# A fifth buffer for split expert weights, with the hand-overs of ScalarE and VectorE one unit on

## The reference

```
logits = h @ w_router;  top_v, top_i = top_k(logits, 2);  gates = softmax(top_v) at top_i
for e in range(8):
    y = y + gates[:, e] * ((silu(h @ w_gate[e]) * (h @ w_up[e])) @ w_down[e])     # 1024 x 3584 each
x = x + y;  return rmsnorm(x, final_norm)
```

## Time and profile before

| | us |
|---|---|
| median of 3 runs | 1400.06 (1399.85 to 1401.4) |
| the profiled execution | 1399.72 |
| its span | 1397.99 |
| TensorE busy in the span | 1367.6 (98%) |
| TensorE's granted clock | 0.998 |

### The profile page before, as it was taken

The page is one execution under the profiler, slowest core; times in us unless marked ns, Lnnn a source line. Parts: engine busy times, 40 slices in busy tenths (PEclk is TensorE's granted clock), DMA queues, the critical chain, the costliest instruction groups (busy, mean ns, idle before and its releaser), DMA issues.

```text
span 1398.0 us, 16748 instructions
## 1 busy us (share of the span) xinstructions
PE 1367.6 (98%) x6662; PEld 1058.6 (76%) x6662; DVE 1103.1 (79%) x858; ACT 925.5 (66%) x723; POOL 51.2 (4%) x51
## 2 busy tenths in 40 slices
PE   9999999999999999999999999999999999999997
PEld 7886788887988888756788866678876668886654
DVE  4786644456455998898998888998888999988898
ACT  3566543344454777777877777787777787777775
POOL 1000000000010000000000000000000000002000
PEclk9999999999999999999999999999999999999999
DMA  9744465555642899999999999999999999999994
GB/s 312 221 157 148 162 210 180 181 180 166 211 149 79 324 361 400 367 376 405 380 406 394 371 390 373 411 383 415 383 358 395 386 399 398 396 381 376 413 403 161
DMA packets 136643, 439.14 MB, mean 314 GB/s; under 512 B 11520, under 2 KB 28912, under 8 KB 120816
## 3 DMA queue, kind: packets, MB, share of 16 engines
q1 hardware_dynamic: 130688, 424.24, 81.1%
q0 software_dynamic: 3392, 12.07, 2.5%
q10 hardware_dynamic: 2480, 1.69, 0.4%
HBM read 432.20 MB, written 5.78 MB: 313 GB/s over the span
## 4 chain that ended last, share of the span: by engine, by line
PE 80%; DVE 15%; ACT 2%; issue 2%; DMA 1%; ACTq 0%; DVEq 0%
PE ps L1879 25%; PE ps L1881 24%; PE ps L1880 24%; DVE lo L1203 9%; PE ps L2427 2%; DVE work L1668 1%; DMA work<-bias_by_distance 1%; PE ps L1939 1%; PE ps L2364 1%; PE ps L2365 1%; DVE work L1229 0%; ACT hi L782 0%; DMA bias_by_distance<-diag_sb 0%; PE ps L2175 0%; DVE x L1657 0%
## 5 line engine op out<-in xcount | busy, mean ns | idle before, releaser
L1203 DVE TENSOR_TENSOR lo<-raw,hi 128x2048 fp32r<-128x2048 f32 (+1 forms) x403 | 903.8, 2282 | 99.9 <-ACT hi L782 98.4
L782 ACT ACTIVATE hi<-raw 128x2048 fp32r<-128x2048 f32 (+1 forms) x403 | 769.1, 1915 | 242.1 <-PE ps L1881 208.2
L1879 PE MATMUL ps<-hi,xT_hi 128*128 128x512 f32 (+2 forms) x1200 | 470.8, 392 | 5.0 <-DVE lo L1203 3.6
L1881 PE MATMUL ps<-hi,xT_lo 128*128 128x512 f32 (+2 forms) x1200 | 465.6, 388 | 0.0
L1880 PE MATMUL ps<-lo,xT_hi 128*128 128x512 f32 (+2 forms) x1200 | 465.4, 388 | 0.0
L1879 PEld LDWEIGHTS ps<-hi,xT_hi 128*128 128x128 f32 (+1 forms) x1200 | 201.7, 168 | 80.7 <-issue 6.9
L1881 PEld LDWEIGHTS ps<-hi,xT_lo 128*128 128x128 f32 (+1 forms) x1200 | 201.4, 168 | 71.4
L1880 PEld LDWEIGHTS ps<-lo,xT_hi 128*128 128x128 f32 (+1 forms) x1200 | 201.6, 168 | 66.7
L1879 PE MATMUL ps<-hi,hT_hi 128*128 128x512 f32 x296 | 116.1, 392 | 0.0
L1881 PE MATMUL ps<-hi,hT_lo 128*128 128x512 f32 x296 | 115.3, 390 | 0.0
L1880 PE MATMUL ps<-lo,hT_hi 128*128 128x512 f32 x296 | 115.2, 389 | 0.0
(11 more groups left out here) (312 smaller groups left out, 942.9 us busy)
## 6 DMA issues: line engine op xcount, KB each, us to landing
raw<-in_od_w_gate_dram SPq DMA_DIRECT2D x112, 1024.0 KB, 8.2
raw<-in_od_w_up_dram SPq DMA_DIRECT2D x112, 1024.0 KB, 8.8
raw<-in_od_w_down_dram SPq DMA_DIRECT2D x112, 1024.0 KB, 8.2
raw<-in_od_w_qkv_dram SPq DMA_DIRECT2D x12, 1024.0 KB, 5.3
raw<-in_ev_w_gate_dram SPq DMA_DIRECT2D x11, 1024.0 KB, 5.3
raw<-in_ev_w_up_dram SPq DMA_DIRECT2D x11, 1024.0 KB, 5.1
raw<-in_ev_w_down_dram SPq DMA_DIRECT2D x11, 1024.0 KB, 5.2
raw<-in_ev_w_in_dram SPq DMA_DIRECT2D x4, 1024.0 KB, 11.0
```

Of the source, the lines that this page charges most:

```text
L782: act.activation(unit(hi, n), unit(raw, n), ACT.Copy).then_inc(hi_ready, 1)
L1203: dve.tensor_tensor(unit(lo, n), unit(raw, n), unit(hi, n).bitcast(F32), ALU.subtract)\
L1879: pe.matmul(out, s_hi, m_hi, start=start, stop=False, skip_group_check=True)
L1881: return pe.matmul(out, s_lo, m_hi, start=False, stop=stop, skip_group_check=True)
```

## The change

The fifth slot (`hi4`, `lo4`) fills the arena. It is used in the branch with gathered tokens; `moe_slots[0]` is set back to 4 while the code of the dense branch is written out. Every `used(k)` of that branch now issues the splits one unit further, on ScalarE and on VectorE, so that each hand-over stands one split later in their orders. The four fetched results go to other rows: the free half of `gain`, `probT`, and two parts of `work`, which held the gathered rows and the stored result. GpSimd waits for one count more (`gathered`, 16) before it fetches. In the dense branch `hd` moves to the first two of these rows.

```diff
@@ constants @@
 HM = 4
+SM = 5
@@ build @@
+    moe_slots = [SM]
+
     def slot_of(n):
-        return n % H if n < U_MOE else (n - U_MOE) % HM
+        return n % H if n < U_MOE else (n - U_MOE) % moe_slots[0]
 
     def frees_slot(n):
         if n < U_MOE:
             return n - H + 1
-        if n >= U_MOE + HM:
-            return n - HM + 1
+        if n >= U_MOE + moe_slots[0]:
+            return n - moe_slots[0] + 1
+        if slot_of(n) == H + 1:
+            return U_MOE
         if slot_of(n) == H:
             return U_WO[1] + 1
...
+        hi4 = nc.alloc_sbuf_tensor_at("hi4", [P, UNIT], F32R, offset=arena_at)
+        lo4 = nc.alloc_sbuf_tensor_at("lo4", [P, UNIT], F32R, offset=arena_at + 4 * UNIT)
...
-        hd = nc.alloc_sbuf_tensor_at("hd", [P, T, D], F32, offset=arena_at)
...
-        results = nc.alloc_sbuf_tensor_at("results", [P, 2 * T, D], F32, offset=arena_at)
+        probT_row = probT[:].rearrange("p t h q -> p (t h q)")
...
-            if slot_of(n) == H:
-                return (hi3 if ring is hi else lo3)[:, 0:a * b]
+            if slot_of(n) >= H:
+                return ((hi3, hi4) if ring is hi else (lo3, lo4))[slot_of(n) - H][:, 0:a * b]
...
         def result_row(i):
-            return results[:, i, :]
+            return (gain[:, 1, :], probT_row, work[:, 2, :], work[:, 3, :])[i]
@@ gpsimd @@
                 pool.wait_ge(slots_ready, 1)
+                pool.wait_ge(gathered, 2 * NE)
                 pool.wait_ge(y_stored, stores_before(NE - 1))
@@ scalar, gathered branch @@
                     def used(k):
-                        splits_to(min(first_of(e) + k + 3, U_END))
+                        splits_to(min(first_of(e) + k + 4, U_END))
@@ vector, gathered branch @@
                     def used(k):
-                        splits_to(min(first_of(e) + k + 2, U_END))
+                        splits_to(min(first_of(e) + k + 3, U_END))
@@ scalar, vector, tensor @@
+            moe_slots[0] = HM
             with act.Else():
...
+            moe_slots[0] = SM
```

More of the change, by code:

```diff
@@ L601, in scatter_bank, with dense_h @@
             return 2 + i if e == NE - 1 else 6
-        def dense_h(c):
-            return hd if c % 2 else work[:, 2:4, :]
+        def dense_h(c, t):
+            return (gain[:, 1, :], probT_row)[t] if c % 2 else work[:, 2 + t, :]
         VARS = [1, 4, 6, 8, 10]
@@ L1839, in dense_pair @@
                             for t in range(T):
-                                dve.tensor_tensor(dense_h(c)[:, t, 0:w], work[:, t, 0:w],
+                                dve.tensor_tensor(dense_h(c, t)[:, 0:w], work[:, t, 0:w],
                                                   ps[:, 4 + 2 * t:4 + 2 * t + w // W, :].rearrange("p a n -> p (a n)"),
@@ L2519, in dense_down @@
                                         ins = pe.transpose(ps[:, 4 + t, P * j:P * j + P],
-                                                           dense_h(c)[:, t, W * b + j:W * b + W:4], ident[:])
+                                                           dense_h(c, t)[:, W * b + j:W * b + W:4], ident[:])
                                 ins.then_inc(hT_done, 1)
```

## The result

| | before | after |
|---|---|---|
| median of each | 1400.73 us (1399.85 to 1403.35, 4 runs) | 1390.05 us (1389.86 to 1391.95, 4 runs) |
| ratio, with its 95% interval | | 0.992 [0.9908, 0.9932] |
| profiled execution, its span | 1399.72, 1397.99 | 1391.95, 1390.1 |
| expert stage in it (end of the last unit before it to the last down matmul) | 445.56 to 1386.44: 940.88 | 449.65 to 1378.59: 928.94 |

The four executions of before are the three known ahead of the prediction and one more, of 1403.35 us. 12.0 was predicted.

A forecast was written before the change was run, and what follows sets the result against it. TensorE, busy 98% of the span, was taken as the bound, losing time to VectorE's late low parts. Gains of 8.9, 2.3 and 0.8 us made 12.0, so 1400.06 became 1388.0 us, range 1385.5 to 1397.

The forecast's parts named there:

- What can be won: Expert stage, 459 to 1386 us: TensorE's lost time sums to 11.8 us, at most 13.3 with uncounted hand-overs.
- The size: Experts 1, 3, 5 and three starts win 8.9 us, expert 7 2.3, small hand-overs 0.8: 12.0.
- Neither works alone: Expert stage: neither the fifth buffer with old orders nor the new orders with four buffers works.
- The head start comes from each split being one unit ahead: Expert stage, buffer and orders together: each split comes one unit ahead, 2.72 to 2.76 us, or 1.81 after a down.
- Part 2, the product behind one more subtraction: VectorE's last product in half-tile experts, behind one more subtraction, stays free: 0, bounds 0 to 2.2 us each.
- Part 3, the results' rows and GpSimd's wait: Results in other rows and one more GpSimd wait before the fetches: cost 0, with 50 us of room.
- The loads have room: Expert stage: weight loads keep up at 414 GB/s, with 10 us to spare per pair of experts.
- The first rival: Expert stage: loads become the bound in part and halve the stage's gain, 1391 to 1397 us; chance 0.17.
- the second, that nothing moves: Queue engines are full, so earlier issue only lengthens the queue: 1399 to 1401 us; chance 0.08.
- The slower rival: Moved hand-overs block ScalarE and VectorE, some 3.6 us per half-tile expert: 1402 to 1412 us; chance 0.08.

The follow-up runs named there:

- Experiment 3: Kernel after with four buffers instead of five, both ScalarE's and VectorE's orders one unit on: 1394.66 us, ratio 0.9948.
- experiment 5: Kernel after with four buffers and ScalarE's hand-overs as before, only VectorE's order one unit on: 1395.1 us, ratio 0.9958.
- 2: buffer: Kernel after with both engines' hand-overs put back, so five buffers and the results' new rows alone: 1401.23 us, ratio 0.9995.
- experiment 6: Kernel after with VectorE's hand-overs put back, so five buffers and ScalarE's order alone one unit on: 1408.52 us, ratio 1.0056.
- 4: VectorE, five: Kernel after with ScalarE's hand-overs put back, so five buffers and VectorE's order alone one unit on: 1391.0 us, ratio 0.9926.
- experiment 8: Kernel before with VectorE subtracting only half of each expert-stage unit from the fifth on, all orders kept: 1387.85 us, ratio 0.9905.
- 9: Kernel after with each expert-stage load bringing only the first half of its unit: 1389.56 us, ratio 0.9916.
- 7: Five buffers, ScalarE's order alone one unit on, each expert-stage load bringing only half its unit: 1401.08 us, ratio 0.9998 to before.
- experiment 1: Kernel after run again unchanged, on two chips: 1389.83 us, ratio 0.9913, and 1389.59 us, ratio 0.9918.
- the fill: Kernel after with extra TensorE matmuls at two waits in layer 0, six near 34 us and two at 134 us: 1388.58 us, ratio 0.9916.

## Why the prediction was right, and where its reasons were not

How far ahead of TensorE the parts of a unit are, in expert 3, shows which engine mattered. Each number is the end of the last matmul of the unit before, less the end of the subtraction (low) or split (high) of this unit, from the timelines; a low part at or below 0 means that TensorE waits or comes without a margin. Experiment 3 has the numbers of 5 to within 0.02.

| | before | 2: buffer | 6: ScalarE | 5: VectorE, four | 4: VectorE, five | after |
|---|---|---|---|---|---|---|
| low, first gate unit of chunk 3 | -0.01 | -0.03 | -0.04 | 0.16 | 1.62 | 1.62 |
| low, third down unit of chunk 3 | -0.63 | -0.62 | -0.63 | 1.65 | 2.47 | 3.10 |
| low, first unit of expert 4 | -0.03 | -0.03 | -0.03 | -0.03 | 0.17 | 0.80 |
| high, third down unit of chunk 3 | 5.16 | 5.19 | 7.00 | 5.16 | 5.20 | 7.00 |
| time, us | 1400.7 to 1401.8 | 1401.23 | 1408.52 | 1395.1 | 1391.0 | 1389.6 to 1390.05 |

- *What can be won: right.* 11.8 and at most 13.3 were counted from the starts of matmuls; the floor that experiment 8 shows lies 13.38 below before. The difference to 11.8 is mostly expert 7: it had 112.36 - 108.51 = 3.85 to lose, where the prediction found 2.9. The rest is about 0.1 in each of the other half-tile experts and in expert 0, and 0.18 at the starts.
- *The size: right.* Predicted 8.9 and 2.3 and 0.8, together 12.0; measured in the stage 11.94. Expert 1 won 3.21 (3.1), 3 and 5 won 2.41 each (2.3), 7 won 2.40 (2.3 of its 2.9), the starts 0.46 each (0.4). What the stage gave beyond 11.2 is 0.74, for which 0.8 had been taken from between 0 and 1.5: that it came so close is luck, and so in part are the 2.3 of expert 7, taken from between 0 and 2.9. The time itself came 2.05 us above 1388.0. The stage accounts for 0.06 of that: the rest is the clock in layer 0 (up to 3.6 us between executions), and the 1400.06 that I set out from was the low end of what before does (1400.73, 1401.83, 1401.52 and 1401.02 as medians of later sets).
- *"Neither works alone": wrong.* This is the step that failed. The buffer alone does nothing, as said. But the orders alone give 6.8 us of the stage, and VectorE's alone gives the same (3, 5). I had costed the new orders by ScalarE, by the ring and by the silu behind it, and had not asked what VectorE's own order does. The rows were there: in the earlier trace rows VectorE idles 1.21 us before the product at 904.51. The next high part was ready before that: ScalarE was last in front of this unit at 901.81 for 1.92 us, so from 903.73 on.

```profile
901.81 1.92 ACT L782 ACTIVATE hi<-raw 128x2048 fp32r<-128x2048 f32 x1 [0.84 <-PE ps L1881]
```

  (ScalarE's timeline in the kernel before.) VectorE began that unit at 905.64. The head start of low parts was limited by VectorE's order and not by the buffers alone; with five buffers it was the order entirely (2).
- *The head start comes from each split being one unit ahead: wrong in its cause.* The table shows that ScalarE's high parts one unit ahead (5.16 to 7.00) give the low parts nothing by themselves (6), and with VectorE's shift only the last 0.63 (4 against after). Added in this sequence, VectorE's order gives 6.75 of the stage's 11.94 us (940.88 to 934.13), the fifth buffer under it 4.28 (to 929.85), and ScalarE's order 0.91 (to 928.94); in another sequence the shares differ, since the buffer first gives 0.25. The right size came from the right sum of waits, and from the right bound (one unit more covers a lack of 1.8), with the wrong engine named. That the total did not need the right engine is luck too: both parts were changed together.
- *Part 2, the product behind one more subtraction: right.* The product starts with the same 1.21 us of idle time before it, so the extra subtraction was done earlier, as said.
- *Part 3, the results' rows and GpSimd's wait: right.* The first fetch is still released by a store, after 7.91 us of waiting (7.60 in the earlier trace rows), so the added wait had long been met:

```profile
1278.48 1.31 POOL L773 DMA_INDIRECT gain<-expert_results,rslot_id  x1 [7.91 <-DMA expert_results<-work]
```

- *The loads have room: right.* They moved at 391 and 397 GB/s in experts 2 and 3, which is 394 over the pair, where 394 had been worked out as needed, ScalarE's waits for them grew as foretold, and halving them changed nothing (9). The first rival is out, and with 10.7 to 12.0 us won so is the second, that nothing moves. The Trainium skill (DMA: Bandwidth & Descriptors, Where 436 GB/s comes from) says that some 358 GB/s per core bind for loads from HBM. The 397 over 109.6 us speak against that for this kernel, which runs on one core. The Trainium skill (HBM Reference, Specifications (TRN2)) says that a core that streams alone measures well above this share. The trace agrees with that, by the same 397.
- *The slower rival: a real mechanism, with the wrong trigger.* I put it where VectorE's product meets one more subtraction and gave it 3.6 us per half-tile expert. It happened where ScalarE stands before a load with a copy of h behind it, in full-tile experts above all, and only if VectorE is not shifted too (6, 7). In the kernel after ScalarE has such waits as well, up to 2.2 us in the execution shown and 2.9 in another, and they cost nothing: they add up to less than half of those in experiment 6, and wherever outside expert 7 one exceeds 0.3 us, the low part of that unit is still done 1.8 us or more before TensorE is through with the unit before. In expert 7 halved loads changed nothing (9). So ScalarE's shift needs VectorE's, and not the other way round (4).

## What to carry to other kernels

Where one engine feeds another through a ring, three numbers bound the head start: the buffers, and the place in the order of each engine that works ahead; count all three, and look for idle time that an engine spends in front of an in-order step while its next independent piece is ready. Here a buffer without the order behind it gave nothing (2), and moving the first engine of the chain alone cost 5.6 us of the stage (6): it wanted its input earlier, and that input's buffer is only freed by the second one. And a program that leaves half of one engine's work out, with every order kept, gives the floor in one run; it is better evidence for the cause than a sum of small waits.

## What was not expected of the hardware

TensorE's granted clock fell to 0.50 in layer 0 in nine of the fourteen profiled executions, and not in others of the same kernel on the same data. At the first place, before the matmuls with `flip` at 35 us, TensorE had waited 1.94 and 1.76 us in the kernel after, 1.80 in experiment 5 and 2.43 in experiment 6 where it fell. It stayed at 1.00 after 1.63 us in the kernel after, but also after 2.01 us in experiment 8, whose layer 0 has the same instructions. So the length of the wait alone doesn't decide it. At the second place, from 133.6 us on, it fell in six executions. In the twelve without the fill a wait of 0.55 us after the matmuls of L2083 stands there, in five with the fall and in seven without; the sixth fall came with the fill. In eight of the nine executions a stretch lasted 3.4 us, in experiment 3 one of 6.8. By the starts in the table of experiment 1 one of 3.4 us costs 1.7 to 1.9 us, more than ScalarE's part of this change, and the stretches move the time of one kernel between 1388.34 and 1391.95 us. What decides it could not be settled.
